# Low halves of weight units on GpSimd: 512 columns per instruction instead of one instruction per unit

## The chip, the cores and the metric

The kernel runs on one core of a Trainium2 chip. The metric is the device time of one execution in microseconds. A core has a matrix engine (TensorE, PE in the rows; PEld is its weight load), a vector engine (VectorE, DVE), an activation engine (ScalarE, ACT), a general engine (GpSimd, POOL) and a queue engine (SyncE, SP) that here only issues DMA transfers. They run side by side and meet at semaphores.

## The reference, cut to what matters

Two small transformer stacks run one after the other on 256 positions of width 1024. Nearly all the arithmetic is a product of activations with a weight matrix that is read once from memory:

```python
def conv_ffn(h, w_up, conv_w, w_down):
    u = causal_dwconv(h @ w_up, conv_w)
    val, gate = u[..., :D_FF], u[..., D_FF:]
    return (jax.nn.silu(gate) * val) @ w_down
...
    z = h @ w_in
    q, k, v, qi, ki, wi, bg, cg, xb = _split(z, EVEN_SIZES)
...
        hid = jnp.square(jax.nn.relu(jnp.einsum('bsd,df->bsf', h, w_up[l])))
        x = x + jnp.einsum('bsf,fd->bsd', hid, w_down[l])
```

The first stack has two layers: an even mixer (top-k attention, called DSA, beside a gated short convolution), an odd mixer (pooling beside a latent attention, MLA), and a convolution FFN behind each. The second stack has one layer with three attentions (FOX, MOBA, stick breaking), gates, a "lift" product per branch, and a squared-ReLU FFN.

## The kernel before, in words

All is float32. A product is made of three passes of TensorE over reduced-precision (fp32r) operands: high half times high half, high times low, low times high. So every weight tile must be split on the chip into a high and a low half.

The weights come in 158 **units**, numbered g = 0 to 157 in the order of use. Most are 128 partitions by 2048 columns (8 row tiles of 256 columns); the 12 lift units, the unit of the forget gate and the 32 up units of the last FFN are 1024 wide; a few are 512, 768, 1280 or 1536 wide. A unit passes through these stations:

- SP loads it into `raw[g % 2]` (two DMAs). The issue waits until GpSimd has finished the unit that lay there before: `sp_.wait_ge(lo_up, before(g) + 1)`, for wide units g - 2.
- ACT copies it to `uh[g % 2]` with rounding (`hi_unit`, L799; in the FFN loops L945). It waits for the DMA and for TensorE to have finished unit g - 2.
- POOL subtracts, `ul = raw - uh` (`lo_unit`, L703; in the FFN loops L738), and counts `lo_up`. This is the line that is changed.
- TensorE multiplies. `unit_cols` and `unit_rows` first do the passes that need only the high half (16 matmuls of 256 columns) and wait for `lo_up` then; the FFN loop (`up`) waits for `lo_up` before its first matmul.

In names of rows, `unit_hi` is `uh`, `unit_lo` is `ul`, `h_hi`/`h_lo` the activations' halves, `bank` a PSUM bank, `x` the residual.

POOL runs a fixed list in program order. Besides the units it splits the FFN's down-projection blocks (`lo_down`, L709 and L741: 128x1024), does two tiny instructions for each normalisation (`power`, L715 and L717) and three 128x512 subtractions for the low half of the activations (`h_low`, L725). In an FFN the list is: unit b+1, down block b, and so on; the first pieces of that list are written out, the rest are a hardware loop.

VectorE has work of its own beside this. Of weight for the change are the lines whose operands both lie in SBUF, or that copy from SBUF to SBUF: L1908 (`restore_rows`, x <- x + att, 128x1024, in each of the first four blocks of FFN 0 and 1), L1878 and L1886 (the last layer norm of the first stack), L1924 (rows scaled before they are transposed) and L2226 to L2241 (rotary embedding of MLA). The order of all queues is written out by hand; nothing is scheduled by a planner.

Of the kernel before, what the change touches and what calls it, by code (L numbers as in the profile page):

```python
# [18 lines left out]
ALU = mybir.AluOpType  # L19
ACT = mybir.ActivationFunctionType  # L20
AX = mybir.AxisListType
F32 = mybir.dt.float32
# [86 lines left out]
def build(nc, W, consts, out):  # L109

    units = []
# [6 lines left out]
    def slot(g):  # L118

        return CHUNKW // 2 * (g // 2 % 2) if units[g]["width"] <= CHUNKW // 2 and units[g]["name"] != "ffn2" else 0  # L120
# [142 lines left out]
    with ctx:  # L263
        def sb(name, shape, dt=F32):
            return ctx.enter_context(nc.sbuf_tensor(name, shape, dt))

        def sem(name):
            return ctx.enter_context(nc.semaphore(name))


        raw = [sb(f"raw{i}", [P, CHUNKW]) for i in range(2)]
        uh = [sb(f"unit_hi{i}", [P, CHUNKW], F32R) for i in range(2)]
        ul = [sb(f"unit_lo{i}", [P, CHUNKW], F32R) for i in range(2)]
# [119 lines left out]
        hi_up, lo_up, hi_dn, lo_dn = sem("hi_up"), sem("lo_up"), sem("hi_dn"), sem("lo_dn")  # L393
# [30 lines left out]
        def full(eng, name):  # L424

            b, _, k = turns[name]
            eng.wait_ge(bank_full[b], k)
            return bank[b]
# [116 lines left out]
        for layer in range(2):  # L545
            for part in range(2):
                r0, at = 24 * part, 37 + 32 * layer + 16 * part
# [147 lines left out]

        @block.gpsimd
        def _(pool):
            def lo_unit(g):
                if g >= NU:
                    return  # L700
                pool.wait_ge(hi_up, g + 1)
                w = slice(slot(g), slot(g) + units[g]["width"])
                nc.gpsimd.tensor_tensor(ul[g % 2][:, w], raw[g % 2][:, w], uh[g % 2][:, w].bitcast(F32),  # L703
                                        ALU.subtract).then_inc(lo_up, 1)

            def lo_down(d):
                pool.wait_ge(hi_dn, d + 1)
                s = d % 2
                nc.gpsimd.tensor_tensor(down[:, s, 1, :], rawd[s][:, :], down[:, s, 0, :].bitcast(F32),  # L709
                                        ALU.subtract).then_inc(lo_dn, 1)  # L710
# [17 lines left out]
            def ffn(f):  # L728
                g0, d0, nb = FFN_G0[f], FFN_D0[f], FFN_NB[f]
                w = units[g0]["width"]  # L730
                lo_down(d0)

                def body(i, k):

                    b = 2 * i + k
                    s = (g0 + k) % 2
                    pool.wait_ge(hi_up, b + (g0 + 3))
                    nc.gpsimd.tensor_tensor(ul[s][:, 0:w], raw[s][:, 0:w], uh[s][:, 0:w].bitcast(F32),  # L738
                                            ALU.subtract).then_inc(lo_up, 1)
                    pool.wait_ge(hi_dn, b + (d0 + 2))  # L740
                    nc.gpsimd.tensor_tensor(down[:, 1 - k, 1, :], rawd[1 - k][:, :], down[:, 1 - k, 0, :].bitcast(F32),  # L741
                                            ALU.subtract).then_inc(lo_dn, 1)

                with pool.Fori(0, nb // 2 - 1) as i:
                    for k in range(2):
                        body(i, k)
                lo_unit(g0 + nb)
                lo_down(d0 + nb - 1)

            nc.gpsimd.memset(half_neg, -0.5).then_inc(pool_chain, 1)  # L750
            for dst, src in STAGED:
                pool.dma_start(dst, src).then_inc(stage_in, 16)
            lo_unit(0)
            lo_unit(1)
            for g in range(2, G_EO[-1] + 2):
                lo_unit(g)
# [439 lines left out]
        def _(pe):  # L1196
# [111 lines left out]
            def first_units(n, gs, rows=False, low_last=False):  # L1308
# [17 lines left out]
                def final(part, mm):  # L1326
                    g, _, w, i = part
                    if i == (TT if rows else w // P) - 1:
                        mm.then_inc(bank_full[4 + g % 2], 1)
# [1041 lines left out]
```

## Time and profile before

| | us |
|---|---|
| median of 3 runs | 1219.51 (1218.22 to 1222.25) |
| the profiled execution, own time | 1214.65 |
| its span | 1212.8 |
| TensorE busy | 1143.7 (94%) |
| TensorE weight load busy | 1039.5 (86%) |
| GpSimd busy | 831.9 (69%) |
| ScalarE busy | 583.9 (48%) |
| VectorE busy | 549.0 (45%) |
| granted TensorE clock, mean | 0.976 |

A busy share is an average over stages. What decides is whether TensorE waits in a stage, and for whom. An idle engine off the path costs nothing.

### The profile page before, as it was taken

How to read it: one execution, taken by the hardware profiler on the slowest of the kernel's cores; microseconds unless marked ns; L12 is line 12 of the kernel's file. 1: busy time of each engine (PE TensorE's matmuls, PEld its weight loads, DVE VectorE, ACT ScalarE, POOL GpSimd, SP SyncE). 2: the span in 40 equal slices, each digit the busy share in tenths (PEclk: the TensorE clock that was granted, in tenths of full speed). 3: DMA queues.
4: the chain of work that ended last, by engine and by line, in shares of the span. 5: the costliest groups of instructions: out<-in, count | busy, mean ns of one | idle time of the engine just before them, and what ended most of it. 6: DMA issues, size and time to landing. Idle time of an engine off the chain costs nothing.

```text
span 1212.8 us, 21761 instructions
## 1 busy us (share of the span) xinstructions
PE 1143.7 (94%) x8143; PEld 1039.5 (86%) x8143; DVE 549.0 (45%) x1125; ACT 583.9 (48%) x878; POOL 831.9 (69%) x289
## 2 busy tenths in 40 slices
PE   6899899999999988999999988999999998999996
PEld 2899798999997877989999858999999987999995
DVE  4567778765568743593233370334111234111113
ACT  0445425545452554445455425556786543454451
POOL 3576559898873633698887637656656776988883
PEclk9899999999998988999999999999999999999998
DMA  9987598999993534497566414444444544666561
GB/s 338 314 278 207 192 306 251 343 334 313 310 305 132 140 94 140 141 310 243 168 196 181 130 35 139 140 140 139 128 151 139 186 146 122 208 190 190 178 188 67
DMA packets 253339, 238.01 MB, mean 196 GB/s; under 512 B 18059, under 2 KB 216512, under 8 KB 253280
## 3 DMA queue, kind: packets, MB, share of 16 engines
q1 hardware_dynamic: 234960, 198.70, 53.0%
q10 hardware_dynamic: 17712, 38.28, 8.9%
q8 instruction: 40, 0.66, 0.2%
q0 software_dynamic: 608, 0.22, 0.1%
q14 instruction: 19, 0.16, 0.0%
HBM read 236.12 MB, written 1.05 MB: 196 GB/s over the span
## 4 chain that ended last, share of the span: by engine, by line
PE 66%; DMA 8%; DVE 7%; ACT 7%; POOL 7%; issue 3%; SPq 1%; ACTq 0%; DVEq 0%; POOLq 0%
PE bank L1209 17%; PE bank L1210 16%; PE bank L1211 16%; POOL unit_lo L703 5%; DMA raw<-in_ev_w_in 4%; ACT unit_hi L799 3%; PE bank L1243 2%; PE bank L1234 2%; DMA ada<-in_ada_w 2%; PE bank L1270 1%; PE bank L1235 1%; PE bank L1263 1%; PE bank L1264 1%; PE bank L1426 1%; PE bank L1385 1%
## 5 line engine op out<-in xcount | busy, mean ns | idle before, releaser
L703 POOL TENSOR_TENSOR unit_lo<-raw,unit_hi 128x2048 fp32r<-128x2048 f32 (+4 forms) x88 | 348.0, 3958 | 228.1 <-ACT unit_hi L799 228.1
L1209 PE MATMUL bank<-h_hi,unit_hi 128*128 128x256 f32 x1152 | 327.4, 284 | 2.9 <-POOL unit_lo L738 2.9
L1210 PE MATMUL bank<-h_lo,unit_hi 128*128 128x256 f32 x1152 | 326.3, 283 | 0.0
L1211 PE MATMUL bank<-h_hi,unit_lo 128*128 128x256 f32 x1152 | 326.2, 283 | 0.0
L738 POOL TENSOR_TENSOR unit_lo<-raw,unit_hi 128x2048 fp32r<-128x2048 f32 (+1 forms) x70 | 257.0, 3671 | 66.3 <-ACT unit_hi L945 64.9
L1209 PEld LDWEIGHTS bank<-h_hi,unit_hi 128*128 128x128 f32 x1152 | 221.2, 192 | 8.6 <-issue 5.6
L1210 PEld LDWEIGHTS bank<-h_lo,unit_hi 128*128 128x128 f32 x1152 | 221.2, 192 | 2.5
L1211 PEld LDWEIGHTS bank<-h_hi,unit_lo 128*128 128x128 f32 x1152 | 221.2, 192 | 0.0
L799 ACT ACTIVATE unit_hi<-raw 128x2048 fp32r<-128x2048 f32 (+4 forms) x98 | 163.2, 1666 | 112.1 <-PE bank L1211 32.8
L741 POOL TENSOR_TENSOR down<-raw_down,down 128x1024 fp32r<-128x1024 f32 x70 | 176.0, 2514 | 0.0
L2027 DVE SCALAR_TENSOR_TENSOR work<-bank,cols,work 128x254 f32<-128x254 f32 (+1 forms) x176 | 72.6, 474 | 139.6 <-ACT work L932 139.5
L1209 PE MATMUL bank<-down,y_hi 128*128 128x512 f32 x304 | 119.7, 394 | 2.0 <-POOL down L709 1.1
L1210 PE MATMUL bank<-down,y_hi 128*128 128x512 f32 x304 | 119.1, 392 | 0.0
L1211 PE MATMUL bank<-down,y_lo 128*128 128x512 f32 x304 | 118.4, 389 | 0.0
L945 ACT ACTIVATE unit_hi<-raw 128x2048 fp32r<-128x2048 f32 (+1 forms) x60 | 90.8, 1514 | 6.7 <-DMA raw<-in_ffn_w_up 6.7
L930 ACT ACTIVATE work<-bank,cols 128x256 f32<-128x256 f32 x44 | 20.9, 474 | 123.0 <-PE bank L1211 109.1
L2056 DVE TENSOR_TENSOR bank<-bank,work 128x256 f32<-128x256 f32 x32 | 13.8, 433 | 132.8 <-ACT work L935 132.8
L1234 PE MATMUL bank<-h_hi,unit_hi 128*128 128x256 f32 x272 | 70.1, 294 | 2.5 <-DVE h_full L2179 2.5
L967 ACT ACTIVATE down<-raw_down 128x1024 fp32r<-128x1024 f32 x60 | 63.3, 1056 | 15.1 <-PE bank L1211 14.3
L1209 PEld LDWEIGHTS bank<-down,y_hi 128*128 128x128 f32 x304 | 57.3, 189 | 14.0 <-issue 2.3
L1235 PE MATMUL bank<-h_lo,unit_hi 128*128 128x256 f32 x272 | 68.4, 288 | 0.0
L1211 PEld LDWEIGHTS bank<-down,y_lo 128*128 128x128 f32 x304 | 57.1, 188 | 12.5
(325 smaller groups left out, 2201.0 us busy)
## 6 DMA issues: line engine op xcount, KB each, us to landing
raw<-in_ffn_w_up SPq DMA_DIRECT2D x88, 512.0 KB, 5.2
raw<-in_w_in SPq DMA_DIRECT2D x60, 512.0 KB, 4.6
raw_down<-in_ffn_w_down SPq DMA_DIRECT2D x44, 512.0 KB, 5.1
ada<-in_ada_w ACTq DMA_DIRECT2D x16, 1024.0 KB, 6.8
raw<-in_w_up SPq DMA_DIRECT2D x64, 256.0 KB, 3.0
raw_down<-in_w_down SPq DMA_DIRECT2D x32, 512.0 KB, 3.5
raw<-in_ev_w_in SPq DMA_DIRECT2D x28, 512.0 KB, 5.2
att<-in_ada_w ACTq DMA_DIRECT2D x14, 1024.0 KB, 8.1
```

The lines of the kernel that those rows point to most:

```text
L703: nc.gpsimd.tensor_tensor(ul[g % 2][:, w], raw[g % 2][:, w], uh[g % 2][:, w].bitcast(F32), ALU.subtract).then_inc(lo_up, 1)
L738: nc.gpsimd.tensor_tensor(ul[s][:, 0:w], raw[s][:, 0:w], uh[s][:, 0:w].bitcast(F32), ALU.subtract).then_inc(lo_up, 1)
L741: nc.gpsimd.tensor_tensor(down[:, 1 - k, 1, :], rawd[1 - k][:, :], down[:, 1 - k, 0, :].bitcast(F32), ALU.subtract).then_inc(lo_dn, 1)
L799: nc.scalar.activation(uh[s][:, w], raw[s][:, w], ACT.Copy).then_inc(hi_up, 1)
L945: nc.scalar.activation(uh[s][:, 0:w], raw[s][:, 0:w], ACT.Copy).then_inc(hi_up, 1)
L967: nc.scalar.activation(down[:, 1 - k, 0, :], rawd[1 - k][:, :], ACT.Copy).then_inc(hi_dn, 1)
L1209: nc.tensor.matmul(o, sh, mh, start=first, stop=False)
L1210: nc.tensor.matmul(o, sh, ml, start=False, stop=False)
L1211: return nc.tensor.matmul(o, sl, mh, start=False, stop=last)
L1234: nc.tensor.matmul(o[:, 0:S], uh[s][:, a], mh[:, kt, :], start=kt == 0, stop=False)
L1235: nc.tensor.matmul(o[:, 0:S], uh[s][:, a], ml[:, kt, :], start=False, stop=False)
L2027: return V.scalar_tensor_tensor(t[:, back:S], bank[4 + s][:, S * j:S * (j + 1) - back], w, t[:, back:S], ALU.mult, ALU.add)
```

## The change

A helper `low_pieces` cuts the subtraction of a unit into instructions of 512 columns when the width is a multiple of 512; other widths (768, 1280) stay one instruction. Only the last piece counts `lo_up`, so everybody who waits for the unit still waits for its last column. `lo_down`, `h_low` and `power` are as they were.

```diff
+            def low_pieces(s, at, width):
+
+                n = width // 512 if width % 512 == 0 else 1
+                for i in range(n):
+                    w = slice(at + width // n * i, at + width // n * (i + 1))
+                    ins = nc.gpsimd.tensor_tensor(ul[s][:, w], raw[s][:, w], uh[s][:, w].bitcast(F32), ALU.subtract)
+                ins.then_inc(lo_up, 1)
+
             def lo_unit(g):
                 if g >= NU:
                     return
                 pool.wait_ge(hi_up, g + 1)
-                w = slice(slot(g), slot(g) + units[g]["width"])
-                nc.gpsimd.tensor_tensor(ul[g % 2][:, w], raw[g % 2][:, w], uh[g % 2][:, w].bitcast(F32),
-                                        ALU.subtract).then_inc(lo_up, 1)
+                low_pieces(g % 2, slot(g), units[g]["width"])
...
                     pool.wait_ge(hi_up, b + (g0 + 3))
-                    nc.gpsimd.tensor_tensor(ul[s][:, 0:w], raw[s][:, 0:w], uh[s][:, 0:w].bitcast(F32),
-                                            ALU.subtract).then_inc(lo_up, 1)
+                    low_pieces(s, 0, w)
```

On POOL, at the start of FFN 1 (its loop begins at the branch), these rows stood before:

```order
L703 TENSOR_TENSOR unit_lo<-raw,unit_hi 128x2048 [waits hi_up]
L709 TENSOR_TENSOR down<-raw_down,down 128x1024 [waits hi_dn]
L744 UNCONDITIONAL_BRANCH
L744 ISA
L738 TENSOR_TENSOR unit_lo<-raw,unit_hi 128x2048 [waits hi_up]
L740 REGISTER_ALU
L741 TENSOR_TENSOR down<-raw_down,down 128x1024 [waits hi_dn]
```

And now, at the same place (the loop's subtraction has moved from L738 into the helper's line, the loop's L741 is now L746):

```order
L703 TENSOR_TENSOR unit_lo<-raw,unit_hi 128x512 [waits hi_up]
L703 TENSOR_TENSOR unit_lo<-raw,unit_hi 128x512 x3
L715 TENSOR_TENSOR down<-raw_down,down 128x1024 [waits hi_dn]
L749 UNCONDITIONAL_BRANCH
L749 ISA
L703 TENSOR_TENSOR unit_lo<-raw,unit_hi 128x512 [waits hi_up]
L703 TENSOR_TENSOR unit_lo<-raw,unit_hi 128x512 x3
L745 REGISTER_ALU
L746 TENSOR_TENSOR down<-raw_down,down 128x1024 [waits hi_dn]
```

One instruction has become four, of which only the first waits. Nothing has moved past anything else.

On POOL, between FFN 1 and the second stack, with the two normalisations (`power`) around a unit, before:

```order
L715 TENSOR_SCALAR small<-small 128x2 [waits var_ready]
L717 TENSOR_TENSOR small<-small 128x2 [waits pool_chain]
L703 TENSOR_TENSOR unit_lo<-raw,unit_hi 128x2048 [waits hi_up]
L715 TENSOR_SCALAR small<-small 128x2 [waits var_ready]
L717 TENSOR_TENSOR small<-small 128x2 [waits pool_chain]
```

And now:

```order
L721 TENSOR_SCALAR small<-small 128x2 [waits var_ready]
L723 TENSOR_TENSOR small<-small 128x2 [waits pool_chain]
L703 TENSOR_TENSOR unit_lo<-raw,unit_hi 128x512 [waits hi_up]
L703 TENSOR_TENSOR unit_lo<-raw,unit_hi 128x512 x3
L721 TENSOR_SCALAR small<-small 128x2 [waits var_ready]
L723 TENSOR_TENSOR small<-small 128x2 [waits pool_chain]
```

The four pieces stand where the unit stood, ahead of the second normalisation. The lists of TensorE, ScalarE, VectorE and SP have the same rows as before apart from line numbers.

## Rows read from the trace of the kernel before

**Rows 1.** The page: busy time of engines.

```profile
PE 1143.7 (94%) x8143; PEld 1039.5 (86%) x8143; DVE 549.0 (45%) x1125; ACT 583.9 (48%) x878; POOL 831.9 (69%) x289
```

**Rows 2.** The chain in order of time, from its start: start us, us, what.

```profile
42.74 4.64 POOL unit_lo L703
47.80 5.30 DMA raw<-in_ev_w_in
...
55.12 4.64 POOL unit_lo L703
...
107.01 4.61 POOL unit_lo L703
...
984.26 4.57 POOL unit_lo L703
```

**Rows 3.** Groups by form, POOL: count | busy us, mean ns of one | idle before.

```profile
L703 POOL TENSOR_TENSOR unit_lo<-raw,unit_hi 128x2048 fp32r<-128x2048 f32 x64 | 294.6, 4606 | 193.4 <-ACT unit_hi L799 193.4
L703 POOL TENSOR_TENSOR unit_lo<-raw,unit_hi 128x1024 fp32r<-128x1024 f32 x15 | 36.0, 2397 | 11.0 <-ACT unit_hi L799 11.0
```

**Rows 4.** Timeline of POOL, two windows: start us, us, engine, line, what.

```profile
183.08 2.55 POOL L725 TENSOR_TENSOR h_lo<-h_full,h_hi 128x512 fp32r<-128x512 f32 x2 [4.66 <-DVE h_full L1850]
185.58 1.73 POOL L725 TENSOR_TENSOR h_lo<-h_full,h_hi 128x512 fp32r<-128x512 f32 x1
```

**Rows 5.** Timeline of POOL at the kernel's start.

```profile
0.25 0.10 POOL L2359 MEMSET const-float32-0.0<- 128x1 f32 x1 [0.25 <-issue]
0.28 0.10 POOL L2359 MEMSET const-float32-1.0<- 128x1 f32 x1
```

**Rows 6.** Timeline of FFN 0 in its steady part: POOL and PE.

```profile
327.44 4.62 POOL L738 TENSOR_TENSOR unit_lo<-raw,unit_hi 128x2048 fp32r<-128x2048 f32 x1 [1.52 <-ACT unit_hi L945]
335.65 0.28 PE L1209 MATMUL bank<-h_hi,unit_hi 128*128 128x256 f32 x1
335.94 4.64 POOL L738 TENSOR_TENSOR unit_lo<-raw,unit_hi 128x2048 fp32r<-128x2048 f32 x1 [1.50 <-ACT unit_hi L945]
```

**Rows 7.** Timeline at the start of FFN 1: POOL, DVE, PE.

```profile
517.35 4.58 POOL L738 TENSOR_TENSOR unit_lo<-raw,unit_hi 128x2048 fp32r<-128x2048 f32 x1
...
518.89 4.12 DVE L1908 TENSOR_TENSOR x<-x,att 128x1024 f32<-128x1024 f32 x1
521.89 3.40 POOL L741 TENSOR_TENSOR down<-raw_down,down 128x1024 fp32r<-128x1024 f32 x1
522.07 0.38 PE L1209 MATMUL bank<-h_hi,unit_hi 128*128 128x256 f32 x1 [1.43 <-POOL unit_lo L738]
```

**Rows 8.** One line's instructions: duration ns min/median/max.

```profile
L1908 DVE TENSOR_TENSOR x<-x,att x12: 1211/2727/4122, 195.8 to 544.3; 128x1024 f32<-128x1024 f32 x12
```

**Rows 9.** Timeline, MLA's rotary embedding: DVE, and PE's waits behind it.

```profile
412.10 4.53 DVE L2237 TENSOR_TENSOR work<-accg,consts 128x64 f32<-128x64 f32 x1
416.66 1.77 DVE L2238 TENSOR_TENSOR work<-work 128x64 f32<-128x64 f32 x1
422.57 0.35 PE L1263 MATMUL bank<-unit_hi,down 128*128 128x256 f32 x1 [1.29 <-DVE down L2254]
...
426.54 0.37 PE L1639 MATMUL bank<-accg 128*128 128x16 f32 x2 [1.35 <-ACT att L1093]
```

**Rows 10.** Timeline between FFN 1 and the second stack.

```profile
705.37 5.01 POOL L703 TENSOR_TENSOR unit_lo<-raw,unit_hi 128x2048 fp32r<-128x2048 f32 x1
706.05 6.60 DVE L1886 SCALAR_TENSOR_TENSOR x<-x,small,att 128x1024 f32<-128x1024 f32 x2
...
714.22 0.71 POOL L717 TENSOR_TENSOR small<-small 128x2 f32<-128x2 f32 x1
```

**Rows 11.** Timeline of PE, a wait for a unit's low half.

```profile
739.18 0.70 PE L1243 MATMUL bank<-h_hi,unit_lo 128*128 128x256 f32 x2 [1.92 <-POOL unit_lo L703]
```

**Rows 12.** Timeline of PE, and a window: last three PEclk, DMA share, GB/s.

```profile
137.56 0.36 PE L1234 MATMUL bank<-h_hi,unit_hi 128*128 128x256 f32 x1 [2.46 <-DVE h_full L2179]
...
137.00:141.00 4.00, 3.44 (x20) 3.47 (x21) 3.27 (x6) 2.39 (x2) 0.48 (x1) 0.70 0.76 262
```

## The prediction

> **What bounds the kernel now.** I read the page first. TensorE is busy for 94% of the span and GpSimd for 69% [rows 1]. So the kernel is bound by TensorE nearly everywhere, and the change can only act where TensorE waits for a low half, or where POOL stands in the chain that ended last.
>
> Then the chain in order of time. From 42.7 to 112 us it goes round a loop: POOL splits a unit, SP reissues the freed buffer, the DMA lands over 5 us later, ACT rounds, POOL splits again [rows 2]. A round takes 12.4 us (42.74 to 55.12), and six units of POOL, the first at 42.74 and the last at 107.01, lie on the path there. After that the chain has seven more of POOL's 2048-wide units, the last at 984.26 [rows 2]: one ahead of each of FFN 0 and 1, the first of FFN 1's loop, and four in the second stack, two of them in its attentions; and two 1024-wide ones in the lift product. TensorE's waits for a low half agree: 1.43 us at the second unit of FFN 1 [rows 7] and as much at that of FFN 0, 1.92 us early in the second stack [rows 11], and shorter ones elsewhere.
>
> In the steady part of an FFN POOL has room. Its period is that of TensorE, 8.50 us (327.44 to 335.94), and it is idle for 1.5 of it, waiting for ACT. The unit ready at 332.06 is taken by TensorE at 335.65, 3.6 us later [rows 6]. In the last FFN the room is alike.
>
> The last thing to see is on VectorE. An addition of two SBUF tiles, L1908, takes 1.21 us at best and 4.12 at worst [rows 8]. The worst one asks at 518.89, while a POOL unit runs, ends at 523.0, about 1.1 us after the unit's end at 521.9 [rows 7], and the 1024-wide POOL instruction behind takes 3.40 instead of 2.40 us [rows 3, 7]. So the two exclude one another for whole instructions, and at an instruction's end the one that waits goes first. That it is turn and turn about shows at 412: L2237 needs 4.53 us, gets its turn at a unit's end, and its successor L2238 at once loses the next turn to a queued 768-wide unit (1.77 us) [rows 9].
>
> **The change part by part.** It removes nothing. It adds three instruction starts to a 2048-wide unit, one to a 1024-wide one, and leaves 768 and 1280 alone.
>
> *What a cut costs.* One instruction takes 4.606 us at 2048 columns and 2.397 at 1024 [rows 3], so 2.16 ns a column and about 0.19 us fixed. Queued one behind another, 512-wide ones start 1.25 us apart and last 1.30 (three start from 183.08 to 185.58, so 2 x 1.25; the first two end at 185.63) [rows 4]. Four pieces are then 3 x 1.25 + 1.30 = 5.05 us, against 4.61 to 4.64: about +0.4 us. I take 0.38, since the nearest rows carry semaphore waits and three of the four pieces don't. Two pieces are 1.25 + 1.30 = 2.55 against 2.40: +0.15, of which I take 0.13. Bounds: at most 4 x 1.30 - 4.61 = +0.59, say 0.55, if nothing overlaps. At least 0, if the fixed part is hidden altogether; the nearest row for that is POOL's memsets without waits, that last 0.10 us and start 0.03 apart [rows 5]. That they are not subtractions makes me stay by the first.
>
> The Trainium skill (GPSIMD Engine Reference, Instruction dispatch) says that each of the eight cores starts the next instruction as soon as it is done with its share of this one, with a dispatch of some tens of cycles in software. By that most of the 0.19 us would be hidden and the cut nearly free, which is the first rival below; the spacing of 1.25 in the row speaks against it.
>
> *The loop of the first stage.* Six units on the path, 6 x 0.38 = +2.3 us. Nothing hides it: the DMA can't be issued before the last piece. It is an upper value in so far as some of the loads take over 5.1 us beside other traffic.
>
> *Start of FFN 0 and of FFN 1.* The unit ahead of the loop and the second unit are late by 0.38 each, and TensorE already waits for the second, so 0.76. Besides, L1908 asks in the middle of the second unit. Before, it had to wait for the unit's end and delayed only the down block. Now it gets its turn at the first boundary between pieces, about 1.1 us on the engine pair, and the unit that TensorE waits for ends 1.1 us later. That is 0.76 + 1.1 = 1.9 us at each FFN, +3.8 together. The later units get the same insertion, but POOL's total work per block, 4.6 + 2.4 + 1.0 + 0.38, is 8.4 us, still under 8.50, so the delay is not added to again. POOL is then late by about 2 us, which the idle 1.5 us per block of the steady part takes up [rows 6].
>
> *Around the normalisation at 706.* L1886 asks at 706.05, in a unit that began at 705.37, and the pair of them takes 6.60 us instead of some 2.5, to go by L1908's best of 1.21 [rows 8, 10]. With pieces the order is piece, L1886, piece, L1886, two pieces: the second L1886 ends near 710.6 instead of 712.65. But POOL's normalisation L717 is queued behind the last piece, which ends near 713.1. So L717 ends at about 714.05 instead of 714.93, and TensorE goes on 0.9 us earlier: -0.9.
>
> *MLA's rotary embedding.* Here the stalls are the longest (4.53 and 1.77 us), yet I cost the edit at nothing. Twelve short additions stand in a row, each wants a turn, and POOL has a piece queued for each. Through four pieces and the 768-wide unit VectorE gets five additions done by 419, where it had two by 418.4; the seven left end near 420.9, as before. If VectorE kept its turn, up to 2.6 us of TensorE's waits behind it (1.29 and 1.35) could go [rows 9].
>
> *The second stack.* The unit for which TensorE waits 1.92 us [rows 11]: +0.4. The two on the chain in the attentions: +0.8. In the lift product two 1024-wide units are on the chain, 2 x 0.13, and behind them the 2048-wide ones of the output projection, the first on the chain at 984.26 [rows 2] and one that hangs on it, 2 x 0.38; with a little for the other lift units +1.2. At 1013 two L1924 and two pieces take turns and the second L1924 ends some 0.1 later; the first loop unit of the last FFN adds 0.1.
>
> *Sum.* 2.3 + 3.8 - 0.9 + 0.4 + 0.8 + 1.2 + 0.2 = +7.8 us, against the profiled execution (span 1212.8, its own time 1214.65) 1222.4. That execution lies 4.9 us below the median of the runs, so I add the sum to the median, 1219.5 + 7.8, and say **1227 us**, 0.6% slower. With 0.26 us a unit (the piece without a wait a little cheaper) the terms per unit shrink to two thirds and the sum is +5.5; with 0.55 it is +10.5.
>
> **The rivals.** *The cut is hidden* (0.0 to 0.1 us a unit, as with the memsets). Then about 1 us for all units together, the insertion of 2.2 in the FFNs and -0.9 at 706 remain: +2.3, about 1222. For it: three of four pieces have no wait. Against it: the spacing of 1.25 [rows 4].
>
> *VectorE gets no turn between pieces*, because a piece without a wait is taken before the last one has let go. Then the stalls are as before: no 2.2 in the FFNs, no -0.9, so +6.5, about 1226, the same side with another cause. Against it, VectorE does get in between two POOL instructions now whose rows overlap by 0.04 us [rows 7].
>
> *The clock.* Behind a wait of TensorE of 2.46 us the granted clock was 0.70 in the next four microseconds [rows 12], so for over half of them it stood at 1.2 GHz, and about 0.3 x 4 = 1.2 us were lost. The wait at an FFN's second unit grows from 1.4 to about 3.3 us. If the clock falls there too: +1.2 each, 1228 to 1230.
>
> *Faster.* The Trainium skill (SBUF — State Buffer, Who interferes with whom) says that VectorE with two SBUF inputs and a GpSimd instruction hold the shared port as a lock for the whole instruction; the rows agree (4.12 us against 1.21). By that rule alone shorter instructions free VectorE sooner, and this is the rival. Its place is 412 to 421 us. If VectorE keeps its turn at every boundary, -2.6 there, -0.9 at 706, -1.0 at 1013, and up to -2.9 where L1908 (4.1 us against 1.2) holds up VectorE ahead of FFN 0's DMAs: -7.4. It decides only if a cut costs under some 0.05 us too and the insertion stays at 2.2: 1219.5 - 7.4 + 2.2 + 0.5, about 1215. Against it are the lost turn of L2238 [rows 9] and TensorE's run without a wait in FFN 0.
>
> **How the numbers follow.** A difference under 0.3% (3.7 us) can't be told from none here. My forecast, pieces at 0.26 to 0.55 with turns, has 0.58; pieces with no turns 0.08; the clock 0.05; the hidden cut 0.22; faster 0.07. A hidden cut is within 0.3%, the first three are slower, except for a low tail of the first. That makes slower 0.70, same 0.23, faster 0.07. The range goes from the hidden cut with something of the stage's slack (1220) to 0.55 a unit with a clock loss (1232).
>
> **What would show it.** In the changed profile POOL's line L703 has 512-wide forms, and consecutive ones start 1.2 to 1.25 us apart; if the spacing is 1.11 to 1.15, the hidden cut holds. L1908 falls from a median of 2.7 to below 2.4 us. TensorE's wait at the second unit of FFN 0 and 1 grows from 1.4 to about 3.3 us. L1886's two take about 4.6 us. L2238 and its successors each take about 1.2 us. The first stage's round of 12.4 us is 0.4 longer. What would make me wrong is above all the spacing, which no row shows for pieces without a wait, and DMA times in the first stage that shrink by what POOL adds.

## The result and the profile after

The changed kernel takes **1229.62 us** (median of five runs, 1226.19 to 1230.6). The kernel before, run beside it, takes 1218.22 (1216.2 to 1222.25). The ratio is 1.0086, 95% interval 1.0061 to 1.0112: 11.4 us by the medians, 10.5 by the ratio. The profiled execution is that of 1229.62 us, with a span of 1227.6.

The page first: busy time of the engines, and the group of the split.

```profile
PE 1148.9 (94%) x8143; PEld 1041.0 (85%) x8143; DVE 537.4 (44%) x1125; ACT 583.6 (48%) x878; POOL 887.3 (72%) x648
...
L703 POOL TENSOR_TENSOR unit_lo<-raw,unit_hi 128x512 fp32r<-128x512 f32 (+2 forms) x517 | 666.2, 1320 | 259.4 <-ACT unit_hi L804 209.8
```

TensorE is as full as before; POOL's sum of busy time is 887.3 us (72%) where it was 831.9 [rows 1]. The lines have moved: the units of the loops, L738 before, are now in L703 with the others, L1908 is L1913, L1886 is L1891, L741 is L746.

**The price of a cut.** The chain in order of time, start us, us, what; and POOL's timeline in two places.

```profile
43.10 5.05 POOL unit_lo L703 x4
...
142.49 5.03 POOL unit_lo L703 x4
```

```profile
196.28 3.81 POOL L703 TENSOR_TENSOR unit_lo<-raw,unit_hi 128x512 fp32r<-128x512 f32 x3
...
202.41 5.96 POOL L703 TENSOR_TENSOR unit_lo<-raw,unit_hi 128x512 fp32r<-128x512 f32 x4
...
526.40 5.97 POOL L703 TENSOR_TENSOR unit_lo<-raw,unit_hi 128x512 fp32r<-128x512 f32 x4
```

Three of one unit's pieces in 3.81 us are two spacings of 1.25 and a last one of 1.30; four mostly take 5.00 to 5.08 where the whole took 4.59 to 4.64 [rows 2, 3]: +0.43. The two at 202.41 and 526.40, the first of each FFN's loop, take 5.96. What got in between shows on VectorE, and TensorE waits for the unit:

```profile
203.54 1.24 DVE L1913 TENSOR_TENSOR x<-x,att 128x1024 f32<-128x1024 f32 x1
208.51 0.57 PE L1214 MATMUL bank<-h_hi,unit_hi 128*128 128x256 f32 x1 [2.99 <-POOL unit_lo L703]
...
527.52 1.25 DVE L1913 TENSOR_TENSOR x<-x,att 128x1024 f32<-128x1024 f32 x1
532.50 0.57 PE L1214 MATMUL bank<-h_hi,unit_hi 128*128 128x256 f32 x1 [2.98 <-POOL unit_lo L703]
```

L1913 now takes 1.25 us where it took 4.12 [rows 7]. TensorE's wait has gone from 1.43 to 2.98. The matmul behind it lasts 0.57 us, and the windows say why (the third value from the end is the granted clock):

```profile
208.50:213.50 5.00, 4.99 (x31) 5.00 (x32) 3.88 (x6) 2.38 (x4) 5.00 (x4) 0.72 1.00 308
532.00:537.00 5.00, 4.50 (x26) 4.50 (x27) 3.24 (x6) 3.02 (x4) 5.00 (x4) 0.66 0.90 280
```

In the kernel before, the five microseconds behind the same wait (it ends at 198.93 there) run at full clock:

```profile
199.00:204.00 5.00, 5.00 (x42) 5.00 (x43) 4.21 (x9) 2.84 (x4) 4.49 (x2) 1.00 0.96 297
```

**Between FFN 1 and the second stack**, POOL and VectorE, the counterpart of [rows 10]:

```profile
717.15 7.42 POOL L703 TENSOR_TENSOR unit_lo<-raw,unit_hi 128x512 fp32r<-128x512 f32 x4
...
717.83 4.39 DVE L1891 SCALAR_TENSOR_TENSOR x<-x,small,att 128x1024 f32<-128x1024 f32 x2
...
724.96 0.72 POOL L723 TENSOR_TENSOR small<-small 128x2 f32<-128x2 f32 x1
```

The two additions take 4.39 us for 6.60, the unit 7.42 for 5.01. POOL's normalisation starts 10.74 us later than before, in a trace that is 11.79 late at that point: about 1 us of the delay is gone.

**MLA's rotary embedding**, VectorE, the counterpart of [rows 9]:

```profile
422.34 1.23 DVE L2242 TENSOR_TENSOR work<-accg,consts 128x64 f32<-128x64 f32 x1
423.60 1.22 DVE L2243 TENSOR_TENSOR work<-work 128x64 f32<-128x64 f32 x1
...
427.35 1.78 DVE L2246 TENSOR_TENSOR work<-work 128x64 f32<-128x64 f32 x1
```

**A load nobody asked about.** In the output projection TensorE has two new waits, 2.42 and 2.89 us, and the chain shows one transfer ahead of them:

```profile
147.95 14.17 DMA raw<-in_ev_w_out
```

It is the load of unit 17, which SP issues behind the low half of unit 15. The issues of both kernels at that place, with KB and mean us to landing; first before, then after:

```profile
raw<-in_ev_w_out SPq DMA_DIRECT2D x2, 512.0 KB, 4.6
ada<-in_ada_w ACTq DMA_DIRECT2D x1, 1024.0 KB, 8.9
```

```profile
ada<-in_ada_w ACTq DMA_DIRECT2D x1, 1024.0 KB, 5.2
raw<-in_ev_w_out SPq DMA_DIRECT2D x2, 512.0 KB, 12.6
```

Before, SP issues it at 145.15 and ACT its three loads (ada, and the two broadcast rows of the layer norm) from 146.54; after, ACT is first (147.00) and SP second (147.54).

**Where the delay builds up.** For each unit the moment of TensorE's first matmul with its low half can be read; the table holds differences of that moment between two traces, in us (worked out from the traces; the last two columns are pairs of experiments below, that differ by the cut alone).

| unit, place | after - before | e6 - e5 | e4 - e7 |
|---|---|---|---|
| 0, start | +0.68 | +1.21 | +0.39 |
| 12, first stage | +1.31 | +1.71 | +1.76 |
| 16, output projection | +0.45 | +1.72 | +1.31 |
| 20, ahead of FFN 0's loop | +7.88 | +4.51 | +1.49 |
| 22, FFN 0 | +10.80 | +6.44 | +4.46 |
| 58, ahead of FFN 1's loop | +8.77 | +1.87 | +0.58 |
| 60, FFN 1 | +11.79 | +4.07 | +3.74 |
| 80, second stack | +11.00 | +2.60 | +1.49 |
| 111, lift product | +14.06 | +7.41 | +3.79 |
| 124, behind it | +14.89 | +10.78 | +5.90 |
| 157, last | +14.72 | +9.23 | +4.75 |

A single pair of traces is not the median: between two traces of one kernel the columns move by some microseconds, for the reasons that experiments 1 to 8 show. The last column is the clearest case: the trace of e4 is its kernel's fastest run (1220.88 us against a median of 1225.29), so the column ends at 4.75 where the medians of that pair are 9.1 apart.

### The profile page after: what moved, and what is told of

Read it like the earlier page. It is cut to its first block, busy times and chain, and to the rows that moved or that the text cites. A ratio compares the mean times of both kernels' runs of the same rounds, so it can differ in the third digit from the quotient of the medians.

```text
span 1227.6 us, 22120 instructions
## 1 busy us (share of the span) xinstructions
PE 1148.9 (94%) x8143; PEld 1041.0 (85%) x8143; DVE 537.4 (44%) x1125; ACT 583.6 (48%) x878; POOL 887.3 (72%) x648
## 4 chain that ended last, share of the span: by engine, by line
PE 66%; POOL 11%; DMA 8%; ACT 7%; DVE 4%; issue 3%; SPq 1%; DVEq 0%; POOLq 0%; ACTq 0%
PE bank L1214 17%; PE bank L1215 17%; PE bank L1216 17%; POOL unit_lo L703 9%; ACT unit_hi L804 3%; DMA raw<-in_ev_w_in 2%; DMA accg<-in_ada_w 2%; PE bank L1248 2%; PE bank L1239 2%; PE bank L1240 1%; PE bank L1275 1%; DMA raw<-in_w_in 1%; DMA raw<-in_ev_w_out 1%; PE bank L1431 1%; PE bank L1268 1%
## 5 line engine op out<-in xcount | busy, mean ns | idle before, releaser
L703 POOL TENSOR_TENSOR unit_lo<-raw,unit_hi 128x512 fp32r<-128x512 f32 (+2 forms) x517 | 666.2, 1320 | 259.4 <-ACT unit_hi L804 209.8
L746 POOL TENSOR_TENSOR down<-raw_down,down 128x1024 fp32r<-128x1024 f32 x70 | 170.9, 2442 | 0.0
L1214 PEld LDWEIGHTS bank<-down,y_hi 128*128 128x128 f32 x304 | 57.4, 189 | 13.5 <-POOL down L715 1.9
L1215 PEld LDWEIGHTS bank<-down,y_hi 128*128 128x128 f32 x304 | 57.4, 189 | 9.1
```

The costliest lines, as they stand in the source:

```text
L703: ins = nc.gpsimd.tensor_tensor(ul[s][:, w], raw[s][:, w], uh[s][:, w].bitcast(F32), ALU.subtract)
L1214: nc.tensor.matmul(o, sh, mh, start=first, stop=False)
L1215: nc.tensor.matmul(o, sh, ml, start=False, stop=False)
```

## Experiments

The theory: the loss is the late end of units for which TensorE waits, by the cut (0.43) and, in the FFNs, by VectorE's turn between pieces (1.0), and TensorE's lower clock behind the longer waits. The rivals: the late load of unit 17 makes most of it; or the cut alone does, and turns and clock are ornament. Except for the three whose loads are moved and the two with a shorter layer norm, the kernels differ from before or after only in which units are cut and how finely, most by a flag of this form. A difference in us that stands behind a ratio is that ratio's; the kernel before has a median of 1220 to 1221 in these series, over 31 to 35 runs.

```diff
-            def low_pieces(s, at, width):
+            def low_pieces(s, at, width, cut=True):
-                n = width // 512 if width % 512 == 0 else 1
+                n = width // 512 if cut and width % 512 == 0 else 1
```

**1. Only the first stage is cut** (units 0 to 18).

```diff
-                low_pieces(g % 2, slot(g), units[g]["width"])
+                low_pieces(g % 2, slot(g), units[g]["width"], g < 19)
-                    low_pieces(s, 0, w)
+                    low_pieces(s, 0, w, False)
```

> Pieces of 512 only in units 0 to 18, the units ahead of FFN 0; all others whole. The changed kernel's trace lost 7.8 us by the last of these units, nearly all of it at units 17 and 18. Theory A, the load of unit 17 (second quarter of the even mixer's output weights) loses its place: POOL finishes unit 15 2.4 us later, so the load is issued behind ScalarE's loads of 147 us instead of ahead of them, and lands 14 us after its issue instead of 5.5. Then this kernel loses 7 to 8 us against before (ratio 1.006), and TensorE waits over 5 us in all around unit 17. Theory B, of the prediction: only the cuts on the path add up, 0.43 each, +1 to +2.6 us (ratio 1.001 to 1.002).

Measured: 1220.55 us against 1220.1, ratio 1.0003 [0.9983, 1.0023]: +0.4 us, at most 2.8. The trace has the late load of unit 17 (7.92 us behind before at unit 18), so the load alone does not make the median.

**2. Only the loops of FFN 0 and 1 are cut.**

```diff
-                low_pieces(g % 2, slot(g), units[g]["width"])
+                low_pieces(g % 2, slot(g), units[g]["width"], False)
-                    low_pieces(s, 0, w)
+                    low_pieces(s, 0, w, f < 2)
```

> Pieces of 512 only in the loops of FFN 0 and 1; all other units whole. Theory A, VectorE's addition gets its turn inside the loop's first unit: TensorE's wait there grows from 1.4 us to about 2.9 (0.43 for the cuts and 1.0 for the addition), the unit takes 6.0 us instead of 4.6, and with about 1 us of TensorE at half clock behind it each FFN loses 2.4: +3 to +5 us in all (ratio 1.0025 to 1.004). Theory B, only the cuts cost: +0.9 us (ratio 1.0007), the unit takes 5.05 us.

Measured: 1223.67, ratio 1.0023 [0.9995, 1.0051], +2.8 us. TensorE loses 4.1 us from unit 20 to 22 and 2.9 from 58 to 60, and waits where it did in the changed kernel:

```profile
205.41 0.58 PE L1214 MATMUL bank<-h_hi,unit_hi 128*128 128x256 f32 x1 [2.83 <-POOL unit_lo L703]
```

What I had not looked for: units 0 to 20 are whole here, as in the kernel before, and the load of unit 17 is late all the same. SP issues it at 147.42, ACT its ada load at 147.31.

```profile
ada<-in_ada_w ACTq DMA_DIRECT2D x1, 1024.0 KB, 6.7
raw<-in_ev_w_out SPq DMA_DIRECT2D x2, 512.0 KB, 10.9
```

**3. Only unit 45 is cut**, that runs beside the rotary embedding.

```diff
+                low_pieces(g % 2, slot(g), units[g]["width"], g == 45)
```

> Pieces of 512 only in unit 45, the one that runs beside MLA's rotary embedding on VectorE; all other units whole. Theory A, VectorE comes forward between the pieces: TensorE gains what the changed kernel's trace gained between its units 45 and 49, 3.6 us (ratio 0.997), and loses at most 0.4. Theory B, the prediction's: turn and turn about leaves VectorE's row of additions no sooner done, 0 to +0.2 us (ratio 1.000).

Measured: 1218.62, ratio 0.9997 [0.997, 1.0024], nothing that can be told. In its trace TensorE gains 3.1 us from unit 46 to 48. VectorE is not the reason: its first L2242 to its first L2259 takes 8.35 us for 8.71, a gain of 0.4. The clock is. Window 430 to 435, before and here:

```profile
430.00:435.00 5.00, 5.00 (x25) 5.00 (x25) 1.48 (x6) 0.60 (x1) 0.00 (x0) 0.50 0.07 15
```

```profile
430.00:435.00 5.00, 5.00 (x38) 4.79 (x37) 1.79 (x6) 3.08 (x7) 1.08 (x1) 1.00 0.04 8
```

And the kernel of experiment 1, in which unit 45 is whole and TensorE's two waits are those of before (1.3 and 1.4 us), has the full clock there too (its window 438 to 443), and the same 3.1 us:

```profile
438.00:443.00 5.00, 5.00 (x38) 4.79 (x38) 1.75 (x7) 2.78 (x6) 0.78 (x1) 1.00 0.10 23
```

**4. The changed kernel, with the layer norm's two broadcast loads issued later** (behind ACT's rounding of unit 17).

```diff
             attention(DSA, even_filler)
-            load_rows(0, W["ln_mix_g"][0:1, :], W["ln_mix_b"][0:1, :])
...
                 other(g)
+                if j == 0:
+                    load_rows(0, W["ln_mix_g"][0:1, :], W["ln_mix_b"][0:1, :])
```

> The changed kernel with one thing more: ScalarE issues the two broadcast loads of the layer norm's rows (1 MB in all) behind its rounding of unit 17 and not ahead of it. Theory A, lost place in the DMA queues: the load of unit 17 now has only one 1 MB load ahead of it instead of 2 MB, and lands about 10 us after its issue instead of 14; TensorE's waits around unit 17 fall from 5.3 to about 1 to 2 us and the kernel comes to 1.005 to 1.006 of before instead of 1.009. Theory B, POOL's longer units alone make the stage late: no change, 1.009.

Measured: 1225.29, ratio 1.0048 [1.0033, 1.0064]. Unit 18 is 0.47 us behind before instead of 7.75. About 4.6 of the 10.5 us are gone (1.0086 to 1.0048), and 5.9 are left; experiment 7 shows that this alone does not make the load a cost of the change.

**5 and 6. Before and after with L1908's scaling and shifting cut to 8 columns.** L1908 and L1913 are one multiplication and one addition per row tile with the layer norm's rows (`att` in the rows). Both kernels leave out nearly all of them. The edit is the same in both:

```diff
-                    V.tensor_tensor(x[:, tt, :], x[:, tt, :], lnrow[:, shift, :], (ALU.mult, ALU.add)[shift]
+                    V.tensor_tensor(x[:, tt, 0:8], x[:, tt, 0:8], lnrow[:, shift, 0:8], (ALU.mult, ALU.add)[shift]
```

> The kernel before, with VectorE's scaling and shifting of the residual rows in the layer-norm helper (L1908, from 1.21 to 4.12 us) cut to 8 of its columns: this leaves out nearly all of that multiplication and addition. It is the partner of the next kernel. By itself it frees VectorE and takes no turn from POOL: 0 to -3 us against before. In its trace, the units of POOL at the second loop position of each FFN (before: 4.6 to 4.7 us) stay at 4.6 us.

> The changed kernel with the same VectorE instructions cut to 8 columns. Theory 1, the insertion: the 512-column pieces of the first unit of each FFN's loop let L1908 in, at about 1.1 us, and TensorE waits for that unit. With 8 columns the insertion is some 0.1 us: that unit takes about 5.05 instead of 5.96 us, and TensorE's delay from the unit ahead of the loop to the one behind it grows by about 1 us instead of 3 at each FFN, so this kernel is some 4 us nearer to its partner than the changed kernel is to before: +5 to +8 in all. Theory 2, the cut itself or the clock: the delay at each FFN stays at 3 us with the unit at 5.05, and the distance stays at 9 to 11 us.

Measured: 1218.7, ratio 0.9982 [0.9957, 1.0007], and 1227.6, ratio 1.0062 [1.0031, 1.0092]. The two are 0.80% apart. The trace of the cut one, POOL, VectorE and TensorE at FFN 0, and the window behind:

```profile
202.96 5.00 POOL L703 TENSOR_TENSOR unit_lo<-raw,unit_hi 128x512 fp32r<-128x512 f32 x4
...
204.07 0.18 DVE L1913 TENSOR_TENSOR x<-x,att 128x8 f32<-128x8 f32 x1
...
208.09 0.38 PE L1214 MATMUL bank<-h_hi,unit_hi 128*128 128x256 f32 x1 [2.02 <-POOL unit_lo L703]
```

```profile
208.00:213.00 5.00, 4.91 (x28) 4.92 (x29) 2.19 (x5) 3.52 (x4) 4.74 (x3) 0.66 0.82 264
```

The unit takes 5.00 instead of 5.96 and TensorE waits 2.02 instead of 2.99: the insertion is shown, at 1.0 us. But the clock fell behind this wait of 2.0 too (0.66), so the delay over the start of an FFN falls only from 3.0 to 1.9 and 2.2 us in the table. "About 1 us" was wrong by the clock. The medians (0.80 against 0.86%) can't tell a gain of 2 us from none.

**7. The kernel before, with the late layer-norm loads** of experiment 4.

> The kernel before, with the two broadcast loads of the layer-norm rows (ACT's queue) issued behind the rounding of unit 17 instead of ahead of the output projection's units. Theory 1: which of ACT's ada and layer-norm loads and SP's load of unit 17 is issued first, at 147 us, is an accident of tenths of a microsecond in the kernel before too, and costs 3 to 5 us where it falls badly, so this kernel lies 0 to 3 us below the median of before and its runs spread less than the 10 us of before (some 6). Then the changed kernel's loss of that place is in part such an accident. Theory 2: the place is lost only because of the change (the cut's delay): then this kernel is within 1 us of before, and spreads as much.

Measured: **1216.17** against 1220.93, ratio 0.9962 [0.9941, 0.9982], a gain of 4.6 us, as much as the same edit gains in the changed kernel. So the late arrival of unit 17 burdens both kernels in some runs, and the medians show no part of it as a cost of the change: between the two kernels with moved loads the ratio is 1.0048/0.9962 = 1.0086, that of the original pair. A share of some 2 us is not excluded. With the loads in their old place it is late in four of four traces whose first stage is cut (in 512 or 1024) and in three of six whose first stage is whole, at 4 to 7 us by unit 18, and the ratios carry 0.2 to 0.3% of uncertainty. The spread, 9.1 us over 12 runs, is within that of the other kernels (8 to 14 over 7 to 12 runs), so that part of theory 1 fell here; experiment 12, with the same loads moved, spreads over 5.7.

**8. The kernel before, unit 15 alone in 16 pieces of 128 columns.**

```diff
+                n = 16 if g == 15 else 1
+                for i in range(n):
+                    c = units[g]["width"] // n
+                    w = slice(slot(g) + c * i, slot(g) + c * (i + 1))
```

> The kernel before, with the low half of unit 15 alone in 16 pieces of 128 columns, which ends it about 2 us later (16 x 0.14 by the 0.14 us of a cut). SP's load of unit 17 is queued behind that low half. Theory 1: a delay of 2 us there always puts the load behind ACT's loads; it lands 14 us after issue instead of 5.5, and TensorE is late by 5 to 8 us at unit 18, 3 to 6 of them still there at the first FFN, +3 to +5 in all. Theory 2: the order at the queues does not matter and the late landing in the changed kernel had another reason: unit 18 late by 2 us or less, +0 to +2 in all.

Measured: 1221.98, ratio 1.0009 [0.9987, 1.0031], and 5.8 us over the kernel with the loads moved. The unit takes 6.71 us, SP issues behind ACT's three loads, and TensorE is 6.4 us later at unit 18 than it was at 16:

```profile
140.60 6.71 POOL L706 TENSOR_TENSOR unit_lo<-raw,unit_hi 128x128 fp32r<-128x128 f32 x16 [4.62 <-ACT unit_hi L802]
...
161.83 0.39 PE L1266 MATMUL bank<-unit_hi,y_hi 128*128 128x256 f32 x1 [1.97 <-ACT unit_hi L802]
166.47 1.21 PE L1273 MATMUL bank<-unit_lo,y_hi 128*128 128x256 f32 x8 [2.47 <-POOL unit_lo L706]
```

Against before, which has this late load in some of its executions, only 1.1 us remain.

**9. Only the units from 79 on are cut**: the second stack, the lift product and the last FFN.

```diff
-                low_pieces(g % 2, slot(g), units[g]["width"])
+                low_pieces(g % 2, slot(g), units[g]["width"], g >= 79)
-                    low_pieces(s, 0, w)
+                    low_pieces(s, 0, w, f == 2)
```

> Only the units from 79 on (the second stack, the lift product and the last FFN) are cut; all before them are whole as before. The changed kernel's trace gives TensorE's delay 11.8 us behind FFN 1 and 14.7 us in the last FFN, so +3 there, and the pair with the shortened layer norm +6 on the same way. Theory 1, the rest of the loss is here: +4 to +6 us against before. Theory 2, the terms of the prediction hold here: -0.9 at the normalisation and +2.6 in the second stack, so +1.7 us.

Measured: 1222.4, ratio 1.0023 [1.0004, 1.0042], +2.8 us. In its trace TensorE gets 1.0 us back at the normalisation (unit 79) and loses 4.4 from there to the end. Two waits carry much of it in this trace; before, they were 1.50 and 1.60 us, and the clock stayed up behind them:

```profile
935.70 1.79 PE L1248 MATMUL bank<-h_hi,unit_lo 128*128 128x256 f32 x8 [1.83 <-POOL unit_lo L703]
...
997.02 1.70 PE L1275 MATMUL bank<-unit_lo,h_hi 128*128 128x256 f32 x8 [1.90 <-POOL unit_lo L703]
```

```profile
936.00:940.00 4.00, 4.00 (x23) 4.00 (x22) 0.00 (x0) 0.00 (x0) 4.00 (x4) 0.57 0.82 252
997.00:1001.00 4.00, 3.98 (x20) 3.98 (x21) 0.00 (x0) 0.00 (x0) 4.00 (x4) 0.57 0.76 240
```

**10. Only units 19, 20 and 41 to 58 are cut.**

```diff
-                low_pieces(g % 2, slot(g), units[g]["width"])
+                low_pieces(g % 2, slot(g), units[g]["width"], g in (19, 20) or 40 < g < 59)
-                    low_pieces(s, 0, w)
+                    low_pieces(s, 0, w, False)
```

> Only units 19 and 20 (ahead of FFN 0's loop) and 41 to 58 (the units between the two FFNs and the two ahead of FFN 1's loop) are cut. Theory 1: TensorE's clock is granted 0.50 behind the waits at the rotary embedding in five of six traces where unit 45 is whole, and in none of the four where it is cut; so cutting here gives back about 3 us, and what the other units cost (0.8 at units 44, 0.4 at 58) leaves -1 to -3 us. Theory 2: the clock there is an accident that does not hang on the cut; then the cost of the waits alone is left, +0.5 to +2 us.

Measured: 1218.92, ratio 0.9993 [0.9972, 1.0013], -0.9 us: between the two theories, and not to be told from none.

**11. Pieces of 1024 columns everywhere.**

```diff
-                n = width // 512 if width % 512 == 0 else 1
+                n = width // 1024 if width % 1024 == 0 else 1
```

> All units that the change cuts, but in pieces of 1024 columns: two pieces for a 2048-wide unit (one cut, about +0.15 us, instead of three, +0.43), and 1024-wide units stay whole. Theory 1, the loss comes from unit ends that are late: the per-unit part falls to a third, the turn that L1908 gets in the first loop unit of the FFNs stays, and so may the lower clock behind it: +3 to +6 us, half of the loss of the changed kernel. Theory 2, the loss comes from VectorE's turns alone: as the changed kernel, +9 to +11.

Measured: 1224.63 against 1220.65, ratio 1.0014 [0.9988, 1.0039]. A 2048-wide unit takes 4.76 (+0.15), the first of FFN 0's loop 5.70:

```profile
192.98 4.76 POOL L703 TENSOR_TENSOR unit_lo<-raw,unit_hi 128x1024 fp32r<-128x1024 f32 x2
...
200.06 5.70 POOL L703 TENSOR_TENSOR unit_lo<-raw,unit_hi 128x1024 fp32r<-128x1024 f32 x2
```

One boundary is as good to VectorE as three, and the clock falls at both FFNs. TensorE loses 2.7 us at each, 0.3 less than with 512, and almost nothing in the second stack (0.3 us from unit 79 to the last). The loss, 4.0 us by the medians and 1.7 by the ratio, is less than half of the changed kernel's, though the interval reaches from none to 4.8.

**12. Late layer-norm loads** as in experiment 4 **and unit 45 cut** as in experiment 3, both in the kernel before.

```diff
-            load_rows(0, W["ln_mix_g"][0:1, :], W["ln_mix_b"][0:1, :])
+                low_pieces(g % 2, slot(g), units[g]["width"], g == 45)
```

> Layer-norm loads issued late (as in the kernel before with late loads, 1216.2 against 1220.9) and unit 45 alone in pieces of 512. Theory 1: the two gains add, 4.7 and 1 to 3, so -5 to -8 us against before, ratio 0.994 to 0.996. Theory 2: the piece at unit 45 gains nothing in the median: -4 to -5, ratio 0.996 to 0.997.

Measured: 1216.44, ratio 0.9961 [0.9945, 0.9976]: the gain of experiment 7 and nothing from unit 45. In its trace the clock is at 0.50 from 430 to 435 although unit 45 is cut.

**The clock over all 14 traces**, at five places where it differs:

| place | whole, or 1024 where said | cut in 512 |
|---|---|---|
| second loop position's wait, FFN 0 and 1 | full in 9 of 9; with 1024 low in 1 of 1 | low in 4 of 4 |
| behind the rotary embedding (430 to 445) | low in 7 of 8 (1024 among them) | low in 1 of 6 |
| lift and output projections (933 to 1004) | full in 10 of 10 (1024 among them) | low in 3 of 4, at two waits each |
| early in the second stack (739 to 758), behind a wait of 1.9 whole, 1.7 cut | low in 7 of 10 (1024 among them) | low in 0 of 4 |
| start of the last FFN (1015 to 1034), behind a wait of 3.0 whole, 1.9 and 0.5 cut | low in 6 of 10 (full with 1024) | low in 0 of 4 |

The last two rows speak for the cut, and they forbid a rule by the length of a wait. The same wait of 3.00 us, with the units there whole, in the kernel before and in experiment 1, and the windows behind:

```profile
1016.81 0.63 PE L1367 MATMUL bank<-consts,att 128*128 128x128 f32 x4 [3.00 <-DVE att L1924]
1017.00:1021.00 4.00, 3.94 (x33) 3.67 (x32) 2.84 (x8) 2.51 (x7) 0.91 (x1) 1.00 0.47 135
```

```profile
1021.67 0.52 PE L1372 MATMUL bank<-consts,att 128*128 128x128 f32 x3 [3.00 <-DVE att L1929]
1022.00:1026.00 4.00, 4.00 (x24) 4.00 (x23) 2.57 (x7) 2.25 (x6) 0.64 (x1) 0.58 0.45 131
```

**The cut apart from the clock.** Three stretches of the second stack, from one unit's first matmul with its low half to another's, in us over the same 14 traces (worked out from them). In the first no trace differs by the clock:

| stretch | whole or 1024, 10 traces | cut in 512, 4 traces |
|---|---|---|
| unit 88 to 107, attentions | 143.7 to 143.9 | 144.3 to 144.4 |
| unit 107 to 124, lift and output | 70.7 to 70.9 | 71.9 with the clock full (1), 74.4 to 75.8 with it low (3) |
| unit 125 to 140, start of the last FFN | 91.4 with the clock full (4), 91.8 to 92.7 with it low (6) | 91.2 |

**The clock over whole executions.** Each execution of the changed kernel and of the experiments, and of the kernel before beside the experiments, has its span and mean granted clock on record. Span times (1 - clock) is an estimate of what the clock took. It is a rough and rather an upper one, since part of the low stretches lies in waits. Differences of means over the runs, in us:

| kernels | time | of it the clock | rest, with standard error |
|---|---|---|---|
| changed kernel (5 runs) against before (98, three chips) | +8.8 | +0.8 | +8.0, 0.9 |
| 4 against 7 | +9.5 | +2.4 | +7.1, 0.5 |
| 6 against 5 | +10.4 | +3.1 | +7.2, 1.2 |
| 1, first stage | +0.1 | -1.6 | +1.7, 0.8 |
| 2, FFN loops | +3.4 | +1.9 | +1.5, 1.1 |
| 10, middle | -0.8 | -3.1 | +2.3, 0.6 |
| 9, second stack | +3.0 | -1.3 | +4.3, 0.8 |

So 7 to 8 of the 9 to 10 us are not the clock's, and without the clock the four parts add up to the whole (9.8, standard error 1.7). With three quarters of that time counted as lost the first three rests are 8.2, 7.7 and 8.0, and the parts add up to 8.8. The falls at the FFNs are in the traces, but elsewhere the cut kernels get part of the clock back. (The five runs of before beside the changed kernel have no clocks on record; against them the means differ by 10.5.)

## Why the prediction was right, and where its sizes were off

Slower was forecast, for the reason that the runs show: queued pieces start 1.25 us apart, and TensorE and the DMA loop wait for unit ends. 1229.62 lies within the range, 2.6 us above the point. The sum of +7.8 is near what the last table gives without the clock (+7 to +8), but in part by luck, since its terms err both ways. By its steps:

- *What a cut costs.* 0.38 was said for four pieces and 0.13 for two; 0.43 and 0.15 measured. The discount for pieces that wait for nothing was unfounded: the sum from the row of the queued instructions [rows 4], 5.05 us, is what the units take. The first rival, the hidden cut, is excluded.
- *The first stage, +2.3.* This term is oversized. Cut alone the stage costs +0.4, at most 2.8, or +1.7 by the estimate without the clock. From unit 0 to 12 the three pairs of the table lose 0.5 to 1.4 us, and up to 16 at most 0.9. What was taken as one loop from 42 to 112 us is a chain through transfers of 5.1 to 7.5 us; in the changed kernel it passes through TensorE from 60.9 to 80 us, so a later POOL was in part absorbed.
- *Start of the FFNs, 0.76 + 1.1 each.* The wait grew by 1.55, to 2.98. Without L1913's turn it grows by 0.6, so the turn is 1.0 (1.1 said) and the two cuts 0.6 to 0.75 (0.76 said). What was missing is the clock, a rival priced at 1.2 us and given 0.05: it happened at both FFNs in all traces whose loops are cut, and the whole is 3.0 us each instead of 1.9. The evidence at hand was one row, a wait of 2.46 us with the clock at 0.70 behind it [rows 12]; here it fell behind 2.0 as well, and in the lift product behind 1.8. I read that row as a case of its own, though the predicted wait of 3.3 was longer.
- *The normalisation, -0.9.* The delay is 11.79 at unit 78 and 11.00 at 79: -0.8, and 0.7 to 1.2 against before in the other three traces with these units cut. Right.
- *Rotary, 0.* VectorE's turns came as described, but the count was one off: behind the first short addition five more are done by 429.1, and six are left, not seven, at 0.26 each. So 0.4 us are gained. Nearly right for VectorE. But the clock behind it is low in seven of eight traces with unit 45 whole or in two pieces and in one of six with it cut, which is 3.1 us in one trace; the medians of experiments 3 and 12 show none of it.
- *Second stack, +2.4, and 0.2.* Cut alone +2.8 with the normalisation's gain in it, so about +3.7. TensorE's waits around [rows 11] grow together from 2.5 us (0.6 and 1.92) to 2.9 (1.26 and 1.68), by the 0.4 that was said. In the attentions the cuts cost 0.7 from unit 88 to 107 in every cut trace (0.8 said). From 107 to 124, where 1.2 were said for the lift and what is behind it, they cost 1.0 in the changed kernel's own trace (14.89 - 13.92), and 3.5 (9.59 - 6.05) in experiment 9, with the clock low at two waits. The last term had the wrong sign: at the start of the last FFN the first L1929 is done sooner, TensorE waits 1.92 and 0.52 us instead of 3.00, and 0.2 us come back, or 0.6 to 1.5 against traces whose clock is low there. So the clock is a missing term in both directions, and over whole executions experiment 9 has no less of it than before.
- *The rival of no turns* is excluded by L1913 at 1.25 us; *faster* failed because a cut is not free and VectorE keeps no more than every second turn.
- *What the text did not see*: the order of two queues at 147 us. It is worth 4 to 7 us by unit 18 in a trace. The medians show no share of it in the result, since the kernel before has it too, but 2 us of it can't be excluded.

The Trainium skill (GPSIMD Engine Reference, Instruction dispatch) says that each core goes on as soon as its own share is done. The spacing of 1.25 us here leaves 0.14 us of every instruction uncovered, down to pieces of 128 columns (6.71 - 4.60 over 15 cuts), so the trace does not agree with what I took from it, that most of the fixed part would be hidden.

The Trainium skill (SBUF — State Buffer, Who interferes with whom) has the two engines block one another for whole instructions. The traces agree, and add who is next: L1913 asks 1.1 us into the unit, ends 1.1 us behind the first piece (204.78 against 203.70), and the second piece takes 2.26 us instead of 1.26.

**What stays open.** By the ratios the four parts (first stage, FFN loops, middle, second stack) add up to 0.42%, give or take 0.44, the whole is 0.86, give or take 0.26, and 0.86 and 0.80 in two other pairs. By the estimate above the difference lies in the clock, which the parts happened to get more of than the whole; whether by chance, or because the waits of one part change the clock of another, these runs can't tell. Nor is it shown what makes the clock fall behind one wait and not behind the same one in the next trace. And of the six traces with whole units up to 18 and early layer-norm loads, three (experiments 2, 5, 9) have the late load and three (before, 3, 10) have not; in the first three the clock was low near 125 us, in the others near 138. The four traces with a cut first stage and the load late, and experiment 8, were low near 125 too. That these hang together is seen, not tested.

## What to carry to other kernels

Cutting an instruction of GpSimd costs 0.14 us a cut even with nothing to wait for, and opens a door at every boundary: VectorE goes in, which is good where VectorE is late and bad where TensorE waits for the unit. List the consumers at both ends before cutting, and give a bound with TensorE's clock for every wait that changes, in both directions: where it fell behind a wait of 1.8 to 3.0 us it cost more than a cut's 0.4 (in the lift and output projections 1.3 to 2.0 us each), but behind a wait of 3.0 us it was full in four of ten traces. Compare it over whole executions before calling it the cause. When two traces differ at a place that the edit doesn't touch, look whether two queues issue within a microsecond of one another there; moving a load that nobody needs yet brought more (0.4%) than any edit of the split.

## What the runs showed of the hardware

- In the same instructions, with the same waits of 1.3 and 1.4 us, TensorE's clock is granted at 0.50 (1.2 GHz) in one trace from 430 to 435 us, and at 1.00 (2.4 GHz) in another. Units 46 to 48 take 14.3 us in the first and 11.2 in the second. Most kernels spread over 8 to 14 us here, and this is up to 3 of it.
- Two 512 KB loads on SP's queue, issued 1.4 us ahead of ACT's loads, land in 4.6 us (mean of the two); issued 0.1 us behind the first of them, in 10.9; 0.2 behind but with 1 MB less on ACT's queue, in 7.5.
- GpSimd's overhead does not shrink with the piece: 0.14 us a cut at 1024, 512 and 128 columns.
- The length of TensorE's wait does not settle its clock: behind the same wait of 3.00 us the granted clock was 1.00 in one trace (1017 to 1021 us) and 0.58 in another (1022 to 1026).
